# Trainium2: adaLN rows by four matmuls on four column groups of the array, two vectors ahead of the first norm and ten spread over the HGRN heads

## The reference, cut to what matters

```python
cmod = jax.nn.silu(c)
for l in range(DEPTH):
    mod = cmod @ p['w_ada'][l] + p['b_ada'][l]
    sh1, sc1, g1, sh2, sc2, g2 = [u[:, None, :] for u in jnp.split(mod, 6, axis=-1)]
    h = rmsnorm(x, p['norm_g'][l, 0]) * (1 + sc1) + sh1
    mix, ... = the mixer of layer l on h      # layer 0: eight HGRN heads
    x = x + g1 * mix
    h = rmsnorm(x, p['norm_g'][l, 1]) * (1 + sc2) + sh2
    x = x + g2 * hier_moe(h, ...)
y = rmsnorm(x, p['final_g'])
```

## Time and profile before

| | us |
|---|---|
| median of 3 runs | 2647.47 (2646.32 to 2650.36) |
| span of the profiled execution | 2648.1 |
| PE busy in it | 2473.5 (93%) |
| DVE, ACT, POOL busy | 782.2, 442.5, 120.0 |
| DMA | 290.67 MB, 110 GB/s over the span |

### The profile page before, as it was taken

How to read it: one execution, slowest core, us unless ns; L and a number is a source line. 1 busy time by engine, 2 the same in 40 slices (tenths; PEclk the granted TensorE clock), 3 DMA queues, 4 the chain that set the end, 5 groups by cost and what they waited for, 6 DMA issues and landing times.

```text
span 2648.1 us, 26856 instructions
## 1 busy us (share of the span) xinstructions
PE 2473.5 (93%) x10008; PEld 1669.8 (63%) x10009; DVE 782.2 (30%) x1701; ACT 442.5 (17%) x674; POOL 120.0 (5%) x193
## 2 busy tenths in 40 slices
PE   8999999999699999989979999999999988999996
PEld 1487878347477788666753654736537755877765
DVE  0134344211511111244563443433432033111112
ACT  0223233210310000121121220312201030000001
POOL 0000000000100000000002011020010010000000
PEclk9999999979779999989989999999999995999998
DMA  9412121651014444221116224062242110344420
GB/s 358 174 58 73 64 73 65 216 190 64 0 48 159 159 162 162 72 83 37 51 43 221 81 98 180 24 229 73 82 165 84 64 40 0 135 159 158 159 88 37
DMA packets 77782, 290.67 MB, mean 110 GB/s; under 512 B 8912, under 2 KB 8912, under 8 KB 76928
## 3 DMA queue, kind: packets, MB, share of 16 engines
q1 hardware_dynamic: 54432, 200.57, 21.9%
q0 software_dynamic: 23264, 88.88, 9.3%
HBM read 241.94 MB, written 47.48 MB: 109 GB/s over the span
## 4 chain that ended last, share of the span: by engine, by line
PE 83%; DVE 7%; DMA 4%; ACT 3%; issue 2%; DVEq 0%; ACTq 0%; POOL 0%; SPq 0%; POOLq 0%
PE ps L409 21%; PE ps L659 15%; PE ps L668 8%; PE ps L437 6%; PE ps L627 4%; PE ps L489 3%; PE ps L865 3%; PE ps L685 3%; PE ps L421 3%; DMA arena<-in_c 2%; PE ps L874 2%; PE ps L858 2%; DMA out_mc_s<-arena 2%; PE ps L837 2%; PE ps L454 2%
## 5 line engine op out<-in xcount | busy, mean ns | idle before, releaser
L409 PE MATMUL ps<-hT,ring 128*128 128x288 f32 x1792 | 452.5, 413 | 14.9 <-ACT hT L939 11.5
L409 PEld LDWEIGHTS ps<-hT,ring 128*128 128x128 f32 x1792 | 343.7, 193 | 112.9 <-issue 12.2
L659 PE MATMUL ps<-arena,ring 128*128 x2048 | 399.4, 356 | 0.0
L659 PEld LDWEIGHTS ps<-arena,ring 128*128 128x128 f32 x2048 | 386.8, 190 | 10.4 <-issue 8.9
L668 PE MATMUL ps<-ring,arena 128*128 128x512 f32 (+1 forms) x512 | 221.0, 592 | 0.0
L409 PE MATMUL ps<-arena,ring 128*128 128x288 f32 x768 | 191.4, 413 | 3.7 <-DVE arena L1808 3.7
L409 PEld LDWEIGHTS ps<-arena,ring 128*128 128x128 f32 x768 | 148.6, 194 | 46.1 <-DVE arena L1808 4.2
L437 PE MATMUL ps<-ring,cols 128*9 128x512 f32 x384 | 169.2, 603 | 8.7 <-DMA ring<-in_wstream 8.1
L668 PEld LDWEIGHTS ps<-ring,arena 128*128 128x128 f32 (+1 forms) x512 | 90.3, 176 | 125.3 <-issue 125.3
L858 PE MATMUL ps<-arena 128*64 128x512 f32 x256 | 123.4, 612 | 17.8 <-DMA arena<-in_c 17.0
L1506 DVE TENSOR_TENSOR arena<-ps,arena 128x224 f32<-128x224 f32 x64 | 25.1, 392 | 359.0 <-PE ps L659 359.0
(11 more groups left out here) (372 smaller groups left out, 2334.1 us busy)
## 6 DMA issues: line engine op xcount, KB each, us to landing
ring<-in_wstream SPq DMA_DIRECT2D x376, 512.0 KB, 3.3
arena<-in_c POOLq DMA_DIRECT2D x64, 512.0 KB, 4.7
out_mc_s<-arena POOLq DMA_DIRECT2D x64, 512.0 KB, 4.0
arena<-in_hg POOLq DMA_DIRECT2D x8, 512.0 KB, 3.9
out_hg_s<-arena POOLq DMA_DIRECT2D x8, 512.0 KB, 2.9
out_mc_p<-arena POOLq DMA_DIRECT2D x16, 256.0 KB, 2.4
xT<-in_xT SPq DMA_DIRECT2D x1, 2304.0 KB, 16.7
x_dram<-xT POOLq DMA_DIRECT2D x1, 2304.0 KB, 9.1
```

Source lines behind the costliest of these rows:

```text
L409: mm = pe.matmul(ps[:, 2 * p + half, 0:TH], ring[:, r, c * P:(c + 1) * P], rhs(k)[:, TH * half:TH * (half + 1)], start=(k == 0), stop=(k = ...
L659: mm = pe.matmul(ps[:, 2 * p, 0:W], ring[:, r, c * P:(c + 1) * P], mo["hs"][:, c, bass.ds(at_g, W)], start=(c == 0), stop=(c == DC - 1))
```

## The change

- The nine columns of `silc` are widened to 32 (the rest zero, set by DVE), and live in the arena. A matmul then writes 32 partitions. `vec_columns` does a whole vector (1024 outputs, eight slots, 16 matmuls): the two halves of 512 outputs and the two parts of a slot go to output partitions 0, 64, 32 and 96 of one bank, each accumulated over four steps. The two parts are added later. The slots of a vector are loaded in an order that fits this.
- ACT copies the bank (128 x 512) to `modrow`, PE turns it by four transposes of 128 x 128 (`vec_turn`), ACT copies what counts to `modpart` (`vec_parts`, two copies), DVE adds the two parts and the bias (`modulation`, now by ranges of vectors).
- Order: vector 0, sums of squares, vector 1, both turns; then one vector a head between `values` and `scan` (vectors 2 to 8 with heads 0 to 6), its turn inside the scan behind the first scan matmuls; vectors 9 (after head 6's scan), 10 (after head 7's scores) and 11 (after head 7's scan). The modulation of vectors 2 to 11 is added on DVE ahead of the first gated sum.
- SP's list follows: eight vector slots after each head's four. POOL's load of `keep` comes after both turns.

```diff
-            for r in range(R):
-                sp.dma_start(ring[:, r, :], wstream[r]).then_inc(slot_full[r], 16)
+            for r in range(R):
+                sp.dma_start(ring[:, r, :], wstream[vec_source(r)]).then_inc(slot_full[r], 16)
             sp.dma_start(xT, io["xT"]).then_inc(x_in, 16)
...
+            for x in range(VEC):
+                stream(R + x, VEC + vec_source(x))
+            for q in range(4):
+                stream(HG_AT + q, SLOTS["hg"] + q)
+            with sp.Fori(0, H // 2 - 1) as i:
+                for u in range(2):
+                    for q in range(4):
+                        stream_from_loop(i, 2 * PER_HEAD, hg_turn(u + 1) + q, ...)
+                    for x in range(VEC):
+                        stream_from_loop(i, 2 * PER_HEAD, hg_turn(u + 1) + 4 + x, ...)
...
             pool.sem_inc(s["sn_kept"].sem, 1)
+            pool.wait_ge(s["turned"].sem, 2)
             pool.dma_start(hg["keep"], io["keep"]).then_inc(keep_in, 16)
-
-            pool.wait_ge(s["turned"].sem, 1)
...
+            def vec_columns(p, freed, turn):
+
+                pe.wait_ge(pair_free[p].sem, freed)
+                for step in range(4):
+                    for half in range(2):
+                        r, ahead = (turn[0] + 2 * step + half) % R, (turn[0] + 2 * step + half) // R
+                        pe.wait_ge(slot_full[r], 16 * (turn[1] + ahead + 1))
+                        for kk in range(2):
+                            at = 32 * (2 * kk + half)
+                            mm = pe.matmul(ps[at:at + 32, 2 * p, :], silc[:, 2 * step + kk, :],
+                                           ring[:, r, kk * 512:(kk + 1) * 512], start=(step == 0), stop=(step == 3))
+                        used.on(mm)
+
+            def vec_turn(p, buf, kept):
+
+                pe.wait_ge(s["rows_kept"].sem, kept)
+                for c in range(4):
+                    mm = pe.transpose(ps[:, 2 * p + 1, P * c:P * (c + 1)], hg["modrow"][:, buf, P * c:P * (c + 1)], ident)
                 s["turned"].on(mm)
...
-            ada_rows(0)
+            vec_columns(0, 1, (0, 0))
             norm_sums(0)
-            turn_ada_rows(0)
+            vec_columns(1, 1, (R, 0))
+            vec_turn(0, 0, 1)
+            vec_turn(1, 1, 2)
...
                 s["upd"].on(mm)
+                if turn is not None:
+                    vec_turn(*turn)
                 pe.wait_ge(s["vx_ready"].sem, h + 1)
...
                     scores(u, i)
-                    values(1 - u, i + u)
-                    scan(u, i)
+                    values(i, u + 1)
+                    vec_columns(0, 6 * i + (6 + 3 * u + 1), (n, 3 * i))
+                    scan(u, i, (0, u, 2 * i + (FIRST + u + 1)))
...
-            scan(0, last)
-            ada_rows(1)
+            vec_columns(0, 6 + 3 * (H - 2) + 1, (n, 0))
+            scan(0, last, (0, 0, FIRST + H - 1))
+            vec_columns(1, 2 * H + 2, (n + VEC, 0))
             scores(1, last)
-            scan(1, last)
-            pe.wait_ge(s["s_ready"].sem, 4 * H)
-            turn_ada_rows(1)
+            vec_turn(1, 1, FIRST + H)
+            vec_columns(0, 3 * H + 2, (n + 2 * VEC, 0))
+            scan(1, last, (0, 0, FIRST + H + 1))
+            vec_columns(1, 2 * H + 3, (n + 3 * VEC, 0))
+            vec_turn(1, 1, FIRST + H + 2)
...
+            def vec_rows(p, buf, slots):
+
+                act.wait_ge(used, slots)
+                s["rows_kept"].on(act.copy(hg["modrow"][:, buf, :], ps[:, 2 * p, :]))
+
+            def vec_parts(p, v, turned):
+
+                act.wait_ge(s["turned"].sem, turned)
+                for kk in range(2):
+                    ...
+                    ins = act.copy(part, src)
+                pair_free[p].on(ins)
...
                     exponentials(h)
-                    evict(u, h + 1, True)
+                    evict(u, h + 1, ahead, True)
+                    vec_rows(0, 1 - u, ahead + PER_HEAD)
+                    vec_parts(0, 2 * i + (FIRST + u + 1), 2 * i + (FIRST + u + 2))
                     head_norm(h)
...
-            modulation(1)
+            dve.wait_ge(pair_free[0].sem, 1 + 3 * H + 2)
+            dve.wait_ge(pair_free[1].sem, 1 + 2 * H + 3)
+            modulation(0, FIRST, 6, (1,))
+            modulation(1, 0, 6, (0, 1))
             gated(used, SLOTS["wo"], 1, USES["wo"], 0, 0, hg["sq"][:, 0:64])
```

More of the change, by code:

```diff
@@ L72, with hg_turn @@
 NSLOT = _at
+NVEC = LAYERS * 6
+VEC = 8
+FIRST = 2
+TAIL = NVEC - FIRST - (H - 1)
+HG_AT = FIRST * VEC
+PER_HEAD = 4 + VEC
+def hg_turn(h):
+    return HG_AT + (4 + PER_HEAD * (h - 1) if h else 0)
 USES = {}
-_at = 2
+_at = 2 * (1 + 3 * H + 2)
 N_HEADB = 26
-for _name, _n in (("ada0", 12), ("hg", 4 * H), ("ada1", 12), ("wo", DC), ("moe0", 2 * DC + 4 * NE),
+for _name, _n in (("wo", DC), ("moe0", 2 * DC + 4 * NE),
                   ("xm", MT), ("b", N_HEADB * MH), ("md", DC), ("moe1", 2 * DC + 4 * NE)):
@@ L183, in build @@
             ("rs", T), ("Sn", NB, P), ("half", H), ("low", H), ("t1", 3, H), ("t2", H),
-            ("keep", T)])
-        modrow = [carve([("rows", 6 * D)], start)[0]["rows"] for start in (0, hg_end)]
+            ("keep", T), ("modrow", 2, 512), ("gap", 400), ("rstd", T), ("modpart", 2, NVEC, DC * NV),
+            ("silc", DC, 32)])
+        silc, rstd = hg["silc"], hg["rstd"]
         mo, _ = carve([
@@ L466, in _, with project, values @@
                 x.base = 1
[L468 removed]
+            pe.wait_ge(small_in, 16)
+            pe.wait_ge(s["silc"].sem, 1)
+            vec_columns(0, 1, (0, 0))
             norm_sums(0)
[L470 to L478 removed]
+            vec_columns(1, 1, (R, 0))
+            vec_turn(0, 0, 1)
+            vec_turn(1, 1, 2)
+            def project(i, first, norm=None):
+                for q, (p, m, per) in enumerate(((0, 1, 3), (1, 1, 2), (0, 2, 3))):
+                    n = hg_turn(first) + q
+                    feature_tile("hg", 3 * i + n // R, [n % R], p, 2 * per * i + (m + per * first + 1), h_rhs, DC,
                                  norm if q == 0 else None)
[L481 to L484 removed]
+            def values(i, first):
+                n = hg_turn(first) + 3
+                pe.wait_ge(pair_free[1].sem, 4 * i + (2 + 2 * first + 1))
+                pe.wait_ge(slot_full[n % R], 16 * (3 * i + (n // R + 1)))
                 for j in range(TJ):
@@ L488, in values @@
                     for c in range(DC):
-                        mm = pe.matmul(dst, hT[:, c, P * j:P * j + m], ring[:, 4 * u + 3, c * P:(c + 1) * P],
+                        mm = pe.matmul(dst, hT[:, c, P * j:P * j + m], ring[:, n % R, c * P:(c + 1) * P],
                                        start=(c == 0), stop=(c == DC - 1))
@@ L1213, in by_seq, with modulation @@
                 return ap.rearrange("p (b t) -> p b t", b=NB)
-            def modulation(layer):
-                dve.wait_ge(s["turned"].sem, layer + 1)
-                V.link(dve, tt(modt[:, layer], shaped(ps[:, 4, 0:48 * NV], 48, NV),
-                               col("bada", LAYERS, 48)[:, layer, :].unsqueeze(2).broadcast_to([P, 48, NV]), ALU.add))
-                for k in range(2):
+            def modulation(layer, v0, v1, which):
+                rows = slice(DC * v0, DC * v1)
+                n = DC * (v1 - v0)
+                parts = [shaped(hg["modpart"][:, kk, 6 * layer + v0:6 * layer + v1, :].rearrange("p a b -> p (a b)"), n, NV)
+                         for kk in range(2)]
+                V.link(dve, tt(modt[:, layer, rows], parts[0], parts[1], ALU.add))
+                V.link(dve, tt(modt[:, layer, rows], modt[:, layer, rows],
+                               col("bada", LAYERS, 48)[:, layer, rows].unsqueeze(2).broadcast_to([P, n, NV]), ALU.add))
+                for k in which:
                     g = col("ng", LAYERS, 2, DC)[:, layer, k, :].unsqueeze(2).broadcast_to([P, DC, NV])
@@ L1255, in _ @@
             dve.wait_ge(small_in, 16)
-            modulation(0)
+            for p in range(2):
+                dve.wait_ge(pair_free[p].sem, 2)
+            modulation(0, 0, FIRST, (0,))
             norm(0)
@@ L1272, in _ @@
             dve.wait_ge(keep_in, 16)
-            uh = USES["hg"] // 2
             def elementwise(u, h):
```

139 lines of the change are left out of this document (77 added, 62 removed).

## The result

The changed kernel takes 2545.73 us (median of four runs, 2542.81 to 2553.19); the kernel before, run beside it, 2647.64. The ratio is 0.9622, with a 95% interval of 0.9605 to 0.9639. The profiled execution took 2544.24 us, span 2542.3, against a span of 2648.1 before: 105.8 us less; by the medians it is 101.9.

The account below looks back on a forecast made before the run. The prediction took PE to bound the heads and the opening, with DMA to spare in the heads and close behind in the opening. 63.3 - 56.7 + 52.3 = 58.9 us saved from 2647.5 gave 2589 us, range 2545 to 2620.

Parts of the forecast that it names:

- The price of a vector: PE time for one vector's 16 matmuls (32 passes): 7.3 us taken, between bounds of 3.4 and 13.7 us.
- four abreast: Rival: passes on four column groups run together, 3.4 us a vector, 4.2 in a head; 2556 us, chance 0.27.
- the forecast's own mechanism: Stagger: second pass waits for its first, sharing time only with the next matmul's first; 17 pass times, chance 0.52.
- Step 1, the opening: Up to the first projection: only two vectors stand ahead, projection at 47.5 instead of 110.76; 63.3 us saved.
- POOL's later load of keep: Opening: load stands behind the second turn, needed some 10 us after the projection's start; costs nothing, uncovered a few us once.
- Step 2, the heads: Seven heads, vectors 2 to 8: 7.3 us a vector plus 0.8 for four transposes, added in full; 56.7 us lost.
- The wait for the copied rows: In heads, transposes wait for ACT's copy, covered by the scan's first eight records: nothing; uncovered some 0.7 us a head.
- Step 3, the end: Head 6's first scan matmul to the output projection: 70.2 us instead of 122.5; 52.3 us saved.
- bare gap: Ahead of the last head's scores: PE waits for the elementwise chain on DVE and ACT, 11 us uncovered.
- The modulation on DVE: Extra additions ahead of the gated sums, under the first output tile's wait: costs nothing; uncovered under 4 us.
- Nothing behind the output projection changes: After the output projection: only the place of weights in DRAM changes, no time saved or lost.
- The rival on the slower side: Passes run one after the other, 13.7 us a vector: 2655 us, chance 0.14; with bare weight loads some 2700, chance 0.07.

Follow-up runs that it names:

- the kernel with the later vector: Changed kernel with a head's vector columns behind the scan's first matmuls and its turn behind the outputs: 2535.3 us, ratio 0.9576.
- the second profile of the kernel after: The changed kernel, unaltered, run again beside three further kernels on one chip: 2546.27 us, ratio 0.9617; its profiled execution took 2555.45 us.
- The spreading alone: Changed kernel with each half's matmuls adding up in one column group, order, places and loads kept: 2625.7 us, ratio 0.9919.

## Why the prediction was right or wrong

The direction was right, and so was the account of what is path and what is cover. The price of a vector, on which it all hung, was the wrong one of the two that were worked out: what happened is the rival *four abreast* (2556). That the time lies in the forecast's range, by 0.7 us, is owed to the range taking in that rival; the forecast's own mechanism had 2575 to 2612. And the time is 10 us below the rival's too: its terms were 67 saved in the opening, 35 lost in the heads, 60 saved at the end and nothing behind (67.4, 38.2, 65.5 and 11.1 in the spans).

**The price of a vector.** The step that failed is "the second pass must wait for its own first, and nothing behind it can go ahead". The second pass does wait for its own first, but the matmul of the next column group goes ahead of it: 3.48 us a vector, where 7.3 was taken. The trace of before had no two neighbours on different groups, so it could not tell; the rival's reason, that four neighbours never share a group, was the one that counted. The chance of 0.27 that it got was too small: the reason against it was an assumption about the stream, not a row.

The Trainium skill, page "TensorE: Matmul & The Clock Gate", section "Part 3: Packing small matmuls", has the side-by-side rule that the rival drew on, and the trace agrees: four abreast cost 3.48 us where a vector in a row cost 13.7, a factor of 3.9. The same section's statement that matmuls start and end strictly in program order does not hold for the passes here: with four matmuls of a group in a row the next group started when four of the first group's eight passes were still to run (the loads at 34.57 above), and a vector took 8.70 us, where a start in strict order would take 12.4. The measurement decides.

**Step 1, the opening**: 63.3 forecast, 67.4 measured. Up to vector 1 it holds to a tenth, in part by luck: the sums began at 23.2, where some 22 was forecast, and took 10.0 us, slower than the 8.0 of before as assumed but not 11, so that they ended at 33.1, where 33 was forecast. The rest, 6.6 us from the end of vector 1 to the projection, was 7.2 in the sum. What differs is vector 1: 3.6 instead of 7.3. That POOL's later load of keep costs nothing agrees with the opening; no wait for it appears among PE's.

**Step 2, the heads**: 56.7 us lost forecast, 38.2 measured, 5.46 a head. Minus the vector's 4.55 in the heads that leaves 0.9 for four transposes and their neighbours, where 0.8 was taken. The wait for the copied rows was rightly costed at nothing (L485 above without idle time). The experiments carry the step: a head grew by the vector's time plus 0.7 to 1.3 us whether a vector took 4.6, 5.2, 5.4, 8.7 or 12.1. PE bounds a head. Even the rival's 4.2 us was a little low; the slots that come last set 4.4 to 4.7, as the kernel with the later vector shows, where it is 3.5.

**Step 3, the end**: 52.3 saved forecast, 65.5 measured. From head 6's scan, term by term: sums at 8.1 (8.4 forecast); scores at 28.7 (28.1), bare gap 14.2 us (11, with a longer vector 9 in it), so the chain of DVE and ACT does come late next; scores to scan 13.5 (15.7: vector 10 took 4.0 instead of 8, and the scores ran at half throughout); scan to sums 8.1 (13.6 and 0.8); from there to the output projection 6.8 (12). The mis-sized term beside the vector is the clock of the last scan: I took it from rows at 0.55, but vector 10, four abreast, stood ahead of it, and the scan ran at 0.97. With vector 10 moved away it ran at 0.50 and took 14.5 us, which is what the forecast had (14.4 with the turn).

**The modulation on DVE**, costed at nothing: DVE's seven operations ran from 499.07 to 502.11, and its next wait, for the first output tile, lasted to 507.31 (after):

```profile
501.61 0.50 DVE L1309 SCALAR_TENSOR_TENSOR amod<-modt,cols 128x72 f32<-128x72 f32 x2
507.31 0.52 DVE L1335 SCALAR_TENSOR_TENSOR xT<-ps,modt,xT 128x288 f32<-128x288 f32 x1 [5.20 <-PE ps L452]
```

**"Nothing behind the output projection changes"**: the rest is 11.1 us shorter in these two profiles. 3.0 of it is the output projection and the first mixture of experts up to the mLSTM (571.9 before, 568.9 after). It starts at full clock after, and before it ran at half for some time (the stretch of before behind the earlier trace rows, and that of after):

```profile
569.00:599.80 30.80, 29.02 (x123) 22.54 (x123) 10.22 (x19) 4.96 (x7) 1.07 (x2) 0.50 0.06 21
```

```profile
493.56:515.00 21.44, 20.10 (x102) 13.81 (x102) 5.58 (x13) 4.55 (x9) 0.00 (x0) 1.00 0.69 256
```

This is the change's doing, and missed: that stretch took 567.5 to 570.0 us in all nine profiles of kernels that spread the vectors, and 571.9 in the two that don't. 6.1 us more lie in the mLSTM's state part (558.5 before, 552.4 after), where PE waits for loads of states. I do not put these down to the change: the same part took 559.6 in the second profile of the kernel after, and 553.8 to 560.8 in the other kernels, none of which touches it. Some 2 us are left unplaced.

So of the 46.9 us by which the spans differ more than forecast, 22.6 come from the vector's price in the opening and the heads (4.1 and 18.5), 13.2 from the end, where vector and clock share them, 3.0 from the clock behind it, and 8 are not the change's or not placed. The medians differ by 101.9 us, not by 105.8, so some 4 us belong to the two executions that were profiled.

**The rival on the slower side** needed vectors of over 13.0 us. The spreading alone came near it: 12.07 us a vector. The rival's line, 10.4 us for each us of a vector, would put it 9.7 us below before (0.93 x 10.4); it was 0.8% or some 20 us below. The line's slope held (from 3.48 to 12.07 us the time rose by 80 us, 9.3 for each), its start was too high.

## What to carry to other kernels

Where a matmul uses few columns, lay neighbours on different column groups of the array, changing the group at least every second float32 matmul (every fourth pass), and let the operands be needed in the order in which they land. A quicker stage first runs into the transfer that feeds it: spread such a stage over stretches that are bound by PE and have DMA to spare, since here either half of the change gave 0.8% and 1.5% and both 3.8%. And before work is moved into an idle stretch of PE, look at what clock the work behind it ran at; that can take the whole gain.

## What the runs showed of the hardware that was not expected

- Passes on other column groups overtake waiting ones: with eight of a group in a row, the next group starts after four. Times of 3.48, 3.52, 5.22, 8.70 and 12.07 us for the same 32 passes, in five orders, follow from four passes held by each group. This is worked out from times and the rows of weight loads; the queue itself is in no row.
- Moving one vector from behind the scores to ahead of them changed which stretch ran at the lower clock, scores or scan, and left the end of the heads as long as it was: 56.9 against 57.1 us.
- The same code's mLSTM state part differed by 7 us between two profiled executions (552.4 and 559.6); what makes the difference is not shown.
